# Sixteen expert slots in each of two blocks summed by VectorE instead of TensorE, in a two-layer hybrid encoder

## The reference, cut to what matters

```
u = jnp.take(u_tab, ex, axis=0)
act = jax.nn.gelu(jnp.einsum('thkd,td->thk', u, hx), approximate=False) * gx
vv = jnp.take(v_tab, ex, axis=0)
return jnp.einsum('thk,thkd->td', act, vv)
```

## Time and profile before

| | value |
|---|---|
| median of three runs | 1741.68 us |
| the profiled execution | 1749.08 us, of which 1747.3 us are the span of the trace |
| granted TensorE clock, mean of the span | 0.967 of 2.4 GHz |
| TensorE matmul busy | 1525.5 us, 87% |
| VectorE busy | 1156.2 us, 66% |
| ScalarE busy | 800.3 us, 46% |
| GpSimd busy | 627.0 us, 36% |
| moved by DMA | 640.76 MB, of it 536.90 MB by the gathers and 102.39 MB by the other queue |
| highest rate in any fortieth of the span | 428 GB/s |

### The profile page before, as it was taken

The page is one execution under the profiler, slowest core; times in us unless marked ns, Lnnn a source line. Parts: engine busy times, 40 slices in busy tenths (PEclk is TensorE's granted clock), DMA queues, the critical chain, the costliest instruction groups (busy, mean ns, idle before and its releaser), DMA issues.

```text
span 1747.3 us, 24266 instructions
## 1 busy us (share of the span) xinstructions
PE 1525.5 (87%) x8788; PEld 857.9 (49%) x8788; DVE 1156.2 (66%) x2834; ACT 800.3 (46%) x2263; POOL 627.0 (36%) x559
## 2 busy tenths in 40 slices
PE   8999688888988898999979998989987988788885
PEld 7988444444433366454434466645542443333422
DVE  5676677777777556878676456567765657666652
ACT  5563444444445447444344435544343444444442
POOL 0010244444454332345344321333444434444440
PEclk9999899999999999999999999999998999999998
DMA  7312499999999999999999997999999999999991
GB/s 304 122 50 75 155 426 427 427 427 421 427 423 427 427 426 381 373 400 393 426 417 427 427 426 297 380 357 361 398 393 393 426 428 426 419 421 427 426 427 55
DMA packets 88820, 640.76 MB, mean 367 GB/s; under 512 B 9856, under 2 KB 9984, under 8 KB 11392
## 3 DMA queue, kind: packets, MB, share of 16 engines
q0 software_dynamic: 73728, 536.90, 74.6%
q1 hardware_dynamic: 14976, 102.39, 14.4%
HBM read 638.20 MB, written 1.05 MB: 366 GB/s over the span
## 4 chain that ended last, share of the span: by engine, by line
PE 47%; DMA 23%; DVE 19%; ACT 7%; issue 2%; POOL 1%; SPq 0%; ACTq 0%; POOLq 0%; DVEq 0%
PE PS L2022 25%; DMA gath<-in_experts,idx 22%; DVE gath L1353 7%; PE PS L1650 4%; PE PS L2092 3%; PE PS L2068 3%; PE PS L2314 2%; ACT diag L771 2%; PE PS L2004 1%; ACT stat L767 1%; PE PS L1666 1%; DMA ring<-in_w_slabs 1%; DVE onehot L1327 1%; DVE picked L1329 1%; DVE chosen L1330 1%
## 5 line engine op out<-in xcount | busy, mean ns | idle before, releaser
L2022 PE MATMUL PS<-gath,diag 128*128 128x512 f32 x2048 | 989.6, 622 | 184.4 <-ACT diag L771 182.9
L497 POOL DMA_INDIRECT gath<-in_experts,idx x512 | 587.3, 1147 | 860.8 <-PE PS L2022 783.6
L1353 DVE CUSTOM_DVE_ANT_0 gath<-gath,xn 128x1024 f32<-128x1024 f32 x512 | 618.1, 1223 | 339.4 <-DMA gath<-in_experts,idx 335.7
L2022 PEld LDWEIGHTS PS<-gath,diag 128*128 128x128 f32 x2048 | 375.4, 195 | 686.6 <-issue 347.5
L791 ACT ACTIVATE stat<-hid 128x1 f32<-128x1 f32 x512 | 103.5, 202 | 606.7 <-DVE hid L1353 600.3
L771 ACT ACTIVATE diag<-cst,stat 128x128 f32<-128x128 f32 x512 | 205.6, 402 | 48.3 <-ACT stat L767 1.5
L767 ACT ACTIVATE stat<-stat,gate 128x1 f32<-128x1 f32 x512 | 150.8, 294 | 18.6
L2092 PEld LDWEIGHTS PS<-hB,ring 128*128 128x128 f32 x672 | 85.2, 200 | 27.3 <-issue 27.1
L1650 PE MATMUL PS<-hTh,high 128*128 128x256 f32 x296 | 89.6, 303 | 2.9 <-DVE hTl L1009 2.4
L2092 PE MATMUL PS<-hB,ring 128*128 128x128 f32 x672 | 85.6, 283 | 6.4 <-DMA ring<-in_w_slabs 6.4
L1650 PE MATMUL PS<-hTh,low 128*128 128x256 f32 x296 | 83.3, 281 | 0.0
(11 more groups left out here) (415 smaller groups left out, 1485.5 us busy)
## 6 DMA issues: line engine op xcount, KB each, us to landing
ring<-in_w_slabs SPq DMA_DIRECT2D x92, 1024.0 KB
gath<-in_experts,idx POOLq DMA_INDIRECT x512
gffn<-in_gain_ffn SPq DMA_DIRECT2D x3, 512.0 KB, 5.7
xres<-in_x SPq DMA_DIRECT2D x2, 512.0 KB, 4.4
out<-xn SPq DMA_DIRECT2D x2, 512.0 KB, 7.4
cst<-in_consts SPq DMA_DIRECT2D x1, 680.0 KB, 10.7
p_raw<-in_p_t SPq DMA_DIRECT2D x1, 512.0 KB, 15.3
gfin<-in_g_final SPq DMA_DIRECT2D x1, 512.0 KB
```

The source lines that it names most:

```text
L497: pool.indirect_dma_start(gath[:, n % NB], None, experts[n // (TB * SLOTS)], bass.IndirectOffsetOnAxis(ap=idx[:, tb, h, k:k + 1], axis=0)) ...
L1353: dve.tensor_tensor_reduce(out=half_row, in0=half_row, in1=xn[:, v % TB], scale=1.0, scalar=0.0, op0=ALU.mult, op1=ALU.add, accum_out=hid[ ...
L2022: ins = mm(PS[:, 2 * (v % TB) + s], diag[:, n % ND], gath[:, n % NB, D + 512 * s:D + 512 * (s + 1)], start=n % SLOTS == 0, stop=n % SLOTS ...
```

## The change

Of each block 1 and 2, the slots 22, 24, ..., 52 are taken out of TensorE's sum: no diagonal matrix is built for them and no product made. VectorE adds them into a buffer `acc` in SBUF. Its instruction for slot `n` stands behind the dot product of slot `n + 1` and waits until ScalarE has weighted slot `n` (`hid_gated`). A second semaphore, `vspent`, counts these sums; whoever frees a buffer waits for `vspent` or for `spent`, according to the slot. When the block ends, VectorE adds `acc` to the residual in one more instruction, ahead of the two that add the banks.

The memory of `acc` is that of `gffn`, so the gain of layer 1 gets another place (`gffB`), which is free only late in the block. SyncE fetches it at the list's place `q` (102), behind a wait for `yg_ready` (VectorE's step `ym`, 90), in place of `csum` (41).

```
+VSLOTS = [SLOTS * u + t for u in (1, 2) for t in range(22, 54, 2)]
+def product_slots(n):
+    return n - sum(v < n for v in VSLOTS)
...
-                if gains < TB and at >= SLOTS * (gains + 1) + AT["csum"]:
-                    sp.wait_ge(x_ready[gains], 6)
-                    sp.dma_start(gffn[:], gain_ffn[1]).then_inc(in_gain, 16)
+                if gains < TB and at >= SLOTS * (gains + 1) + AT["q"]:
+                    sp.wait_ge(yg_ready, 2 + gains + 1)
+                    sp.dma_start(gffB[:], gain_ffn[1]).then_inc(in_gain, 16)
...
+                if n in VSLOTS:
+                    return
+                q = product_slots(n)
+                if q >= ND:
+                    act.wait_ge(spent, q - ND + 1)
                 act.wait_ge(hid_gated, n + 1)
-                act.activation(diag[:, n % ND], ident, ACT.Copy, scale=c).then_inc(diag_made, 1)
+                act.activation(diag[:, q % ND], ident, ACT.Copy, scale=c).then_inc(diag_made, 1)
...
+            def vector_spend(n):
+                i = VSLOTS.index(n)
+                row, c = gath[:, n % NB, D:2 * D], hgel[:, n % ND:n % ND + 1]
+                dve.wait_ge(hid_gated, n + 1)
+                if i == 0 or VSLOTS[i - 1] // SLOTS < n // SLOTS:
+                    dve.tensor_scalar(acc[:], row, c, None, ALU.mult).then_inc(vspent, 1)
+                else:
+                    dve.wait_ge(vspent, i)
+                    dve.scalar_tensor_tensor(acc[:], row, c, acc[:], ALU.mult, ALU.add).then_inc(vspent, 1)
...
+                    if n - 1 in VSLOTS:
+                        vector_spend(n - 1)
...
-                dve.wait_ge(spent, SLOTS * (u + 1))
+                dve.wait_ge(spent, product_slots(SLOTS * (u + 1)))
+                if any(v // SLOTS == u for v in VSLOTS):
+                    dve.wait_ge(vspent, sum(v // SLOTS <= u for v in VSLOTS))
+                    link(dve.tensor_tensor(xres[:, tb], xres[:, tb], acc[:], ALU.add))
...
+                    if n not in VSLOTS:
+                        q = product_slots(n)
+                        pe.wait_ge(diag_made, q + 1)
```

More of the change, by code:

```diff
@@ L269, in hybrid_encoder @@
         gffn = place("gffn", R + 7648, [D])
+        acc = place("acc", R + 7648, [D])
         sgm = place("sgm", R + 7648, [D])
@@ L283, in hybrid_encoder @@
         rkB = place("rkB", F, [4, P])
+        gffB = place("gffB", F, [D])
         gBs = [place(f"gB{b}", R + D * b, [4, P]) for b in range(TB)]
@@ L342, in hybrid_encoder @@
         rows_ps, rows_ready, gate_ps, sgm_ready, ple_ps = (sem(n) for n in ("rows_ps", "rows_ready", "gate_ps", "sgm_ready", "ple_ps"))
-        uq_ps, values_ps = sem("uq_ps"), sem("values_ps")
+        uq_ps, values_ps, vspent = (sem(n) for n in ("uq_ps", "values_ps", "vspent"))
         bq_ready, in_evac, r_mixed, r_scaled, mixed = (sem(n) for n in ("bq_ready", "in_evac", "r_mixed", "r_scaled", "mixed"))
@@ L369, in hybrid_encoder, with wait_spent @@
         dve_step, act_step, pool_step = sem("dve_step"), sem("act_step"), sem("pool_step")
+        def wait_spent(engine, n):
+            if n in VSLOTS:
+                engine.wait_ge(vspent, VSLOTS.index(n) + 1)
+            else:
+                engine.wait_ge(spent, product_slots(n) + 1)
         block = ctx.enter_context(nc.Block())
@@ L495, in upto @@
                     if n >= NB:
-                        pool.wait_ge(spent, n - NB + 1)
+                        wait_spent(pool, n - NB)
                     pool.indirect_dma_start(gath[:, n % NB], None, experts[n // (TB * SLOTS)], bass.IndirectOffsetOnAxis(ap=idx[:, tb, h, k:k + 1], axis=0)).then_inc(landed[n % NB], 16)
@@ L767, in weight @@
                 act.activation(c, c, ACT.Copy, scale=gate[:, u % TB, h, k:k + 1]).then_inc(hid_gated, 1)
-                if n >= ND:
-                    act.wait_ge(spent, n - ND + 1)
+                if n in VSLOTS:
+                    return
+                q = product_slots(n)
+                if q >= ND:
+                    act.wait_ge(spent, q - ND + 1)
                 act.wait_ge(hid_gated, n + 1)
-                act.activation(diag[:, n % ND], ident, ACT.Copy, scale=c).then_inc(diag_made, 1)
+                act.activation(diag[:, q % ND], ident, ACT.Copy, scale=c).then_inc(diag_made, 1)
             def queries_taken(u, h):
@@ L790, in upto @@
                     act.wait_ge(dot_made, n + 1)
+                    if n - ND in VSLOTS:
+                        wait_spent(act, n - ND)
                     act.activation(hgel[:, n % ND:n % ND + 1], hid[:, n % (TB * SLOTS):n % (TB * SLOTS) + 1], ACT.Gelu).then_inc(gel_made, 1)
@@ L1586, in mix @@
                 dve.wait_ge(xn_ready, 12 + 4 * b)
-                link(dve.tensor_tensor(xn[:, b], xn[:, b], gffn[:], ALU.mult))
+                link(dve.tensor_tensor(xn[:, b], xn[:, b], gffB[:], ALU.mult))
                 at("keys")
@@ L2019, in upto @@
                     v, h, j = n // SLOTS, n % SLOTS // TOPK, n % TOPK
[L2020 to L2024, removed]
+                    if n not in VSLOTS:
+                        q = product_slots(n)
+                        pe.wait_ge(diag_made, q + 1)
+                        for s in range(2):
+                            ins = mm(PS[:, 2 * (v % TB) + s], diag[:, q % ND], gath[:, n % NB, D + 512 * s:D + 512 * (s + 1)],
+                                     start=n % SLOTS == 0, stop=n % SLOTS == SLOTS - 1, skip_group_check=True)
+                        ins.then_inc(spent, 1)
                     if v == 0 and h + 2 < PH:
```

## The result

The changed kernel takes 1746.88 us (median of 20 runs) against 1742.17 us for the kernel before in the same rounds (20 runs). The ratio is 1.0024, with a 95% interval of 1.0014 to 1.0034: the change makes the kernel 4 us slower. That is less than the half per cent that was named as the bound, but it is more than the measurement's uncertainty, and it points the other way from the 1731 us that were forecast.

A forecast was written before the change was run, and what follows sets the result against it. The stretch's first half was taken to wait for TensorE and DMA, its second for VectorE. Block 1's 3.7 plus block 2's 8.3 less 1.0 for additions gave 11.0 us: 1741.7 to 1730.7, called 1731; 8-in-10 range 1715 to 1751.

The forecast's parts named there:

- I cost that at nothing: Gain's load at its new place, a wait and one slab behind it: cost nothing; leaving its old place: 0.5 us won per block.
- The first three terms: Block 1: 0.8 us won up to the exponentials, 0.8 from two ScalarE diagonals, 1.8 from an earlier LORA product.
- Between 0 and 2.7 I take 2.0: Block 1 before the logits: with five products gone, VectorE's shorter wait for scores wins 2.0 us, of 2.7 at most.
- The 1.8 us for the LORA product: Block 1: without slot 38's product and its tile, TensorE's LORA product starts up to 1.8 us sooner; 1.8 taken.
- The last term: Block 1, slot 40 to 53: `ao` 3.1 us earlier, five sums cost 6.1, waits swallow 2.8; 0.2 us lost.
- Block 2: Score waits 5.0 us won, ScalarE's diagonals 0.8, slot 38's product 2.0, gain vector 0.5, second half nothing lost; 8.3 in all.
- The additions of `acc`: At slot 2 of blocks 2 and 3, between 0 and 2 x 1.22 us; 1.0 us lost in all.
- The slower one: Slots 42 to 53: VectorE's sums wait for ScalarE, 1.9 us each; 5.3 and 3.7 us lost, time 1753; chance 0.23.
- Its own point of decision: Slower rival decides once a sum with its wait exceeds 1.03 us and the first half gives less than that excess.
- The DMA rival: DMA hides TensorE's relief, so the first half gains nothing in either block; 5.2 us won, 1736.5; chance 0.14.
- The clock: Thinned TensorE gets a lower clock: four new gaps at some 1.7 us leave 4.2 us won, 1737.5; chance 0.06.

The follow-up runs named there:

- block 1 only: Against the kernel before: VectorE sums only block 1's 16 slots, both gains at the new place, loaded two slabs later in SyncE's queue; 1749.08 us, ratio 1.0044.
- the load behind two slabs: Gain at its new place, loaded two slabs later in SyncE's queue than in the change: without VectorE sums 1744.52 us (1.0007), with all 32 1743.72 us (0.9996).
- the two kernels with short sums: Sums and `acc` additions cover 8 of 1024 columns: the change with all 32 slots, 1732.30 us (0.9945); block 1 only, 1743.87 us (1.0006).
- block 2 only: Against the kernel before: VectorE sums only block 2's 16 slots; block 1's gain loaded as before, block 2's two slabs later than in the change; 1735.50 us, 0.9956.
- the second look at before: The kernel before, unchanged, run again for a second profile; 1743.04 us.
- block 1 with short sums: As block 1 only, but each sum and the addition of `acc` cover 8 of 1024 columns; 1743.87 us, ratio 1.0006.

## Why the prediction was wrong, step by step

**The gain's load.** The step that failed first is "I cost that at nothing". It named the queue and the wait, and then counted only whether the bytes could arrive in time: 1.5 MB in 25 us. It did not ask what the slab behind the wait had done before. There, two slabs went out one by one as their places in the ring came free; the wait turned them and the gain into one burst. With the 0.5 us forecast as won in each block, the term was +1.0 and measured -4.0 us (interval 2.3 to 5.9 lost).

**Block 1.** Forecast 3.2 us won without the load's part; measured 6.4 us lost. The first three terms, 3.4 us won, failed together: slots 20 to 44 take 96.1 us in block 1 only, against 94.7 with the load behind two slabs. "Between 0 and 2.7 I take 2.0" should have been 0: the prediction had the gather's wait in hand and still took the larger part. The sums' own time is not what held the logits: in the two kernels with short sums they start at 652.1 and 652.2 us, no sooner, and VectorE waited 3.7 us for the last gather ahead of them. The 1.8 us for the LORA product came out as 0.65, and the slab behind it was later, not earlier.

The last term, 0.2 us lost, measured 4.1: between slots 44 and 60, 48.8 us against 44.7 in the four kernels without sums or the clock's wait there. Against the two with that wait it is 2.0 and 2.6. Its sum can be redone from rows. The five sums cost 6.4 us at 1.28 us each, where 6.1 was forecast. The 3.1 us by which `ao` was to come earlier did not arrive: it comes 9.2 us after `kmax`, where it came 8.9 us after it, and with short sums 9.5. TensorE, with two products fewer, waited there for ScalarE instead (1.70 us ahead of a tile, none before). And of the 2.8 us of waits to swallow, the 1.87 us stand only where the clock was low: in two executions of six, and there as 1.87 and 1.32. What is left to swallow is 0.94 us at `ao` and 0.91 at `kkn`: 6.4 - 1.85 = 4.6 us, near the 4.1.

**Block 2.** Forecast 7.8 us won without the load's part; measured 7.7 us (block 2 only against before, its addition of `acc` included). The size is right, in part by luck, for its parts are not: against the second look at before, 5.9 us come between slots 20 and 44 (106.2 to 100.3), where 7.8 were forecast, and 2.3 us between 44 and 60, where nothing was. There VectorE had two waits, for TensorE at `ao` and for the key scores, that a sum can stand in.

**The additions of `acc`.** They have no run of their own; they lie within the block terms above.

The three measured terms give -4.0 - 6.4 + 7.7 = -2.7 us, against 4.2 us of loss measured (2.4 to 5.9 by the interval). Each term has an uncertainty of 2 to 4 us, so the sum agrees, but a further term of that size could hide in it. A second sum agrees too: with the load behind two slabs, -1.2 - 6.4 + 7.7 = 0.1 us won, where the change with that load won 0.7 (0.9996).

**The rate.** The prediction has DMA at 426 to 428 GB/s in most of the span; the page of the profile has it there in 18 of 40 slices. No term hangs on it, since the stretches were read window by window.

**The rivals.** The slower one named the place (slots 42 to 53) and the loss of block 1 (5.3 us), but with a wrong price and for both blocks: VectorE hardly waits for ScalarE; the sum's own 1.28 us is enough where no wait is left to take it. Its own point of decision, 1.03 us a sum, had been passed by the forecast's own 1.22; the forecast escaped it only through a first half that was to pay. The DMA rival was right on block 1's first half, where DMA stood at 426 GB/s before and after. The clock was lower in more windows (0.83 and 0.87 in block 1), but block 1 with short sums has such a window too and loses nothing.

What stays open is the rest of the load's price, 1.2 us behind two slabs. It may lie in block 2: slots 100 to 104 take 15.5 to 16.2 us there in three of the five kernels with the load behind slabs, and 13.0 to 14.0 in all others. Open too is why the first half of block 1 gains so little even with short sums. Its slots 20 to 44 take 91.6 and 92.7 us there against 92.9 to 94.7 without sums, and no run here separates the slab's late landing from ScalarE's full queue.

## What to carry to other kernels

Move work to an engine only in the stages where that engine waits, block by block: the same sixteen sums won 7.7 us in one block and lost 6.4 in another that looks alike, since in one VectorE's waits were there to be filled and in the other not. When a load moves in an in-order issue queue, list the transfers behind its wait, see when they went out before, and price their being held back; that the bytes can still arrive in time is no answer where DMA is full. Look for a second profile before a wait of one or two microseconds goes into a sum: one such wait here was there or not with the clock that TensorE was granted.

## What the runs showed of the hardware

A sum with a weight and an accumulator, all fp32 in SBUF, takes VectorE 1.28 us for 1024 columns, more than the 1.22 us of the two-input operation from which it was priced. The first of each block, a product with the weight alone, takes 0.75 us. The Trainium skill, "VectorE: DVE Perf Modes", section "The perf-mode tier table", puts one-input fp32 operations a tier above two-input ones; the 0.75 us against the 1.22 us of the two-input operation agree.

GpSimd waited 47.5 us, in 15 gathers, for VectorE's sums to give a buffer back, up to 7.4 us at a time. A buffer that TensorE's steady queue had freed became bound to a queue with the mixer's steps in it. Its waits for a free buffer became no longer in all: 741.1 us with those for the sums, 783.6 us before. In block 1 only, the waits for sums are 34.5 us, and 22.2 us with short sums, which lose nothing. What they cost by themselves was not tried.
